# Two-layer diffusion trunk on one core: pairing a wide expert and a small expert in one slot-by-slot visit

## The chip, the cores and the metric

One program runs on one core of a Trainium2 chip. The metric is device time in microseconds (us) from the start to the end of an execution. Where the profile speaks of a span, it means the time from the first to the last recorded instruction of one profiled execution.

## The reference, cut to what matters

Two layers of a backbone over 128 context and 256 latent tokens (384 rows of 1024 values, float32). Each layer has a mixing part and a channel part. The channel part of layer 0 is a dense SwiGLU; that of layer 1 sends every row to 2 of 8 experts. Only the experts are touched here:

```python
def moe_swiglu(h, router, w_gate, w_up, w_down):
    probs = jax.nn.softmax((h @ router).astype(jnp.float32), axis=-1)
    top_p, top_i = lax.top_k(probs, TOP_K)          # TOP_K = 2 of 8
    top_p = top_p / jnp.sum(top_p, axis=-1, keepdims=True)
    combine = ...                                    # weight of each expert for each row
    a = jnp.einsum('bsd,edf->bsef', h, w_gate)       # 1024 x 1408 for each expert
    u = jnp.einsum('bsd,edf->bsef', h, w_up)
    hid = jax.nn.silu(a) * u * combine[..., None]
    return jnp.einsum('bsef,efd->bsd', hid, w_down)  # 1408 x 1024
```

An expert has 3 x 1024 x 1408 float32 weights, 17.30 MB. Eight of them are 138.4 MB, and each is read once in this run.

## The kernel before, in words

**The stages.** The kernel runs the mixing part and the dense channel part of layer 0, the mixing part of layer 1, then routes the rows and runs the experts, and at the end gathers each row's two results, sums, scales and stores them. The experts take the last quarter of the span. TensorE (PE) does the products into eight PSUM banks; ScalarE (ACT) and VectorE (DVE) prepare operands and empty banks; SyncE's queue (SP) issues the loads of weights; GpSimd (POOL) scatters the rows to `xslots` in DRAM and gathers them from `yslots`.

**Wide and small visits.** A wide visit takes up to 128 rows of one expert, a small one ("side" in the code) up to 64. `VISITS` (L50) lists the first visits as pairs (wide item, small item):

```python
VISITS = ((0, None), (None, 0), (1, 1), (None, 2), (2, 3))
```

So the order is: wide 0 alone; small 0 alone, with an expert of its own; wide 1 together with small 1, which are two batches of rows of the same expert; small 2 alone; wide 2 together with small 3. After these come wide 3, 4 and 5 in a loop on every engine. `BY_RANK` (L59) gives each expert a place by the number of its rows: the two least used experts go to the visits that are only small, and two busy ones get a wide and a small place. In this run there are six wide and four small batches of rows.

**Slots.** The weights of a visit come in ten slots (j = 0 to 9), each a load of at most 2 MB (2048 KB). Slots 0 to 5 hold gate and up (`M_GU` = 6): two slots for each of three blocks of columns, 512, 512 and 384 wide. Slots 6 to 9 hold down (`M_DN` = 4): 6 or 5 tiles of 128 rows by one half (512) of the 1024 output columns. The weights live in five places (`M_SLOT` = 5), four in `ring` and one in `oT`; slot j sits in place j mod 5, and SP waits until the use of slot j - 5 is over before it issues the load of slot j (L855 to L875, through `used_in`, L831, and `m_used`, L702). SP works in order: what it waits for holds up all later loads.

**A wide slot.** Products of a wide visit take three passes of reduced float32: `m_upper` (L712, ACT) writes the upper part of the weights to one of two tiles, `w_upper_a` and `w_upper_b`; `m_lower` (L718, DVE) writes the rest over the raw weights in their place; `product` (L1634) has PE multiply upper by upper, upper by lower and lower by upper. A slot's work on ACT and DVE goes in parts (`M_PART`); `ahead` (L2140) makes the upper part of slot j + 2 once slot j has been multiplied. `gate_silu` (L2135, ACT) and `hidden_gate` (L2811, DVE) form the hidden values of a block, `turn_hidden` (L1708, PE) turns them, `hidden_upper` (L2130) and `hidden_lower` (L2804) split them. `gathered` (L2124 and L2781) splits the rows of the next visit, which `next_rows` (L1683, PE) has turned.

**A small slot.** `side_slot` (L1646) multiplies by the raw float32 weights, without a split, two groups of 64 PE columns side by side. `side_silu`, `side_gate`, `side_turn` and `side_copy` (L2156, L2786, L1674, L2163) form and turn its hidden values. In a shared visit the small batch uses a slot's raw weights two slots ahead of the wide batch, since DVE overwrites them afterwards (`half_lower`, L2816, waits for the small batch's use).

**Order on the engines.** There is no scheduler: each engine's order is written by hand, in `side_visit` and `main_visit` (L1695 and L1717) for PE, `side_visit` and `item_upper` (L2179 and L2197) for ACT, `side_visit` and `item_lower` (L2794 and L2821) for DVE. Each engine executes in its order and waits at semaphores. A visit's result goes from PSUM to `ytok` by `out_half` (L2147, ACT) in two halves, and SP stores it when it comes to `store_out` (L820), at slot 5 of the next visit. Right before the first small load, SP waits for the scatter of the rows (`moved`, L849).

Of the kernel before, what the change touches and what calls it, by code (L numbers as in the profile page):

```python
# [28 lines left out]
P = 128  # L29
# [20 lines left out]
VISITS = ((0, None), (None, 0), (1, 1), (None, 2), (2, 3))  # L50
# [8 lines left out]
BY_RANK = ((0, None), (1, 1), (2, 3), (3, None), (4, None), (5, None), (None, 2), (None, 0))  # L59
# [122 lines left out]
def build(nc, cst_d, x_prompt, x_sample, cache_k, cache_v, state_in, c, c_ctx, ada_w, ada_b, norms, w_in, qk_norm,  # L182
# [3 lines left out]
    with ctx:  # L186
# [199 lines left out]
        side_x, side_ht = v3(H[:, 0:SIDE * KT], KT), v3(H[:, 512:512 + SIDE * FE], FE)  # L386
        side_h, side_sg, side_xs = H[:, 1216:1472], H[:, 1472:1728], H[0:SIDE, 1728:1728 + D]
# [62 lines left out]
        GU_BANK, TURN_BANK, OUT_BANK = ((0, 1), (6, 7), (0, 1)), (2, 3, 2), (3, 2)  # L450
        SIDE_ROWS, SIDE_DOWN = 6, (7, 6)
# [3 lines left out]
        turns = []  # L455
        for v, (item_v, side_v) in enumerate(VISITS):
            n_item, n_side = VISITS[v + 1] if v + 1 < len(VISITS) else (FIRST, None)
            rows_v = ["rows"] if n_side is not None else []
            hidden_v = [(side_v, b) for b in range(3)] if side_v is not None else []
            turns += hidden_v[0:2] + [("rows", n_side)] * len(rows_v) + hidden_v[2:] if item_v is None else hidden_v + [("rows", n_side)] * len(rows_v)  # L460

        def side_bank(s, b):

            alone = [item for item, x in VISITS if x == s][0] is None
            return B[((0, 1, 0) if alone else (4, 5, 4))[b]]
# [9 lines left out]

        def turned(*key):

            return FG + turns.index(key) + 1
# [4 lines left out]

        def following(v):

            return VISITS[v + 1] if v + 1 < len(VISITS) else (FIRST, None)

        def rows_in_by(v):

            n_item, n_side = following(v)  # L490
            items = [x for x, _ in VISITS[1:v + 1] + ((n_item, n_side),) if x is not None]
            sides = [x for _, x in VISITS[1:v + 1] + ((n_item, n_side),) if x is not None]
            return 16 * len(items) + 16 * len(sides)

        def visit_of(i):

            return VISITS.index([x for x in VISITS if x[0] == i][0]) if isinstance(i, int) and i < FIRST else i + NE - N_FIX
# [149 lines left out]
        slots = []  # L647
        for item_v, s in VISITS:
            if item_v is None:
                slots += [(s, j) for j in range(M_GU + M_DN - 1)] + [(s + 1, 0), (s, M_GU + M_DN - 1), (s + 1, 1)]  # L650
            elif s is not None:
                slots += [(s, j) for j in range(2, M_GU + M_DN)]

        def m_place(j, split=False):

            if j % M_SLOT == M_SLOT - 1:
                return (otS if split else OT)[:, 0:SLOT]
            k = slot(U_MOE + j % M_SLOT)
# [3 lines left out]
        M_PART = ((1, 1, 2), (2, 2), (2, 2), (2, 2), (2, 2), (2, 2), (3, 3), (3, 2), (3, 3), (3, 2))  # L662
# [9 lines left out]
        def m_shape(j):  # L672

            return (2, 4, 512 if j < M_GU - 2 else 384) if j < M_GU else (1, 6 - j % 2, 512)

        def m_first(j):

            return 4 * (j % 2) if j < M_GU else 6 * (j % 2)
# [33 lines left out]
        def m_upper(act, j, h, i):  # L712

            if h == 0:
                act.wait_ge(m_sem(j), m_full(j, visit_of(i)))
            nc.scalar.activation(m_half(w_upper[j % 2], j, h), m_half(m_place(j), j, h), ACT.Copy).then_inc(mw_hi, 1)  # L716

        def m_lower(eng, op, j, h, i, done):  # L718

            eng.wait_ge(mw_hi, M_IT * i + parts_to(j) + h + 1)  # L720
            op.tensor_tensor(m_half(m_place(j, True), j, h), m_half(m_place(j), j, h), m_half(w_upper[j % 2], j, h).bitcast(F32),  # L721
# [9 lines left out]
        def m_sem(j):  # L731
# [2179 lines left out]
```

## Time and profile before

| what | value |
|---|---|
| median of 3 runs | 1925.7 us (1922.33 to 1929.22) |
| profiled execution, its own time | 1921.34 us |
| its span | 1919.5 us |
| mean granted TensorE clock | 0.971 |
| PE busy | 1785.3 us (93%) |
| DVE busy | 1002.3 us (52%) |
| ACT busy | 787.2 us (41%) |
| POOL busy | 257.6 us (13%) |
| chain that ended last | PE 81%, ACT 5%, DVE 5%, DMA 5% |

The profiled execution lies 4.4 us under the median of the runs. Outside the span lie 1.8 us. Busy time of an engine is an average over stages; the trace can be asked for single stretches, given in us from the start of the span.

### The profile page before, as it was taken

The page shows a single profiled execution, that of the slowest core. Times are in us where ns is not written, and L with a number is a line of the kernel's source. Part 1 is how long each engine was busy: PE and PEld are TensorE (multiplying, and loading weights), DVE is VectorE, ACT ScalarE, POOL GpSimd, SP SyncE. Part 2 cuts the span into 40 slices and gives each one's busy share as a digit, 9 for nine tenths or more (in the row PEclk, how much of TensorE's full clock was granted, in tenths as well). Part 3 has the DMA queues.
Part 4 walks back from the last instruction along what each step waited for, and adds up shares of the span by engine and source line. Part 5 has one row for each costly group of instructions (what it writes and reads, how often), then busy time and mean ns, then how long its engine had stood idle before and what let it go on. Part 6 is the DMA issues. An engine that isn't in the chain of part 4 may idle for free.

```text
span 1919.5 us, 32369 instructions
## 1 busy us (share of the span) xinstructions
PE 1785.3 (93%) x14036; PEld 1503.8 (78%) x14036; DVE 1002.3 (52%) x1290; ACT 787.2 (41%) x1094; POOL 257.6 (13%) x221
## 2 busy tenths in 40 slices
PE   5999899999989999998998999999988799899994
PEld 3888688887869999877997788888867356468884
DVE  2866345444745443337963445546448044257885
ACT  3345622234344222224365422325345143347774
POOL 2610033231000000005300223320002000000001
PEclk9999899999999999998999999999999999899997
DMA  9652052216552344337521412226458978959994
GB/s 350 221 196 94 1 210 67 89 46 209 176 197 71 126 131 131 132 135 259 209 88 50 165 64 93 89 89 219 172 212 297 376 253 287 373 191 335 374 381 146
DMA packets 186387, 350.74 MB, mean 183 GB/s; under 512 B 5097, under 2 KB 60417, under 8 KB 185744
## 3 DMA queue, kind: packets, MB, share of 16 engines
q1 hardware_dynamic: 182464, 335.01, 49.5%
q0 software_dynamic: 3792, 13.80, 2.0%
q8 instruction: 104, 1.70, 0.4%
q14 instruction: 27, 0.22, 0.0%
HBM read 319.43 MB, written 29.36 MB: 182 GB/s over the span
## 4 chain that ended last, share of the span: by engine, by line
PE 81%; ACT 5%; DVE 5%; DMA 5%; SPq 2%; issue 2%; POOL 0%; POOLq 0%; DVEq 0%; ACTq 0%
PE bank L1100 6%; PE bank L1671 5%; PE bank L1102 5%; PE bank L1101 5%; PE bank L1640 5%; PE bank L1641 5%; PE bank L1643 5%; PE bank L1528 3%; PE bank L1526 3%; PE bank L1527 3%; PE bank L1136 3%; PE bank L1138 3%; PE bank L1137 3%; PE bank L1341 2%; PE bank L1478 2%
## 5 line engine op out<-in xcount | busy, mean ns | idle before, releaser
L1102 PE MATMUL bank<-hT_hi,ring_split 128*128 128x384 f32 x576 | 196.1, 340 | 0.0
L1777 ACT ACTIVATE ring_split<-ring 128x1024 fp32r<-128x1024 f32 (+2 forms) x84 | 119.5, 1440 | 180.1 <-DMA ring<-in_ffn_w_up 102.5
L2635 DVE TENSOR_TENSOR ring_split<-ring,ring_split 128x2048 fp32r<-128x2048 f32 (+1 forms) x28 | 73.9, 2670 | 142.7 <-ACT ring_split L1777 142.7
L1100 PE MATMUL bank<-hT_hi,ring_split 128*128 128x384 f32 x384 | 142.4, 371 | 4.3 <-DVE modv L2306 2.9
L721 DVE TENSOR_TENSOR ring_split<-ring,w_upper_a 128x1536 fp32r<-128x1536 f32 (+2 forms) x54 | 96.5, 1814 | 76.9 <-PE bank L1671 68.7
L1138 PE MATMUL bank<-ring_split,hT_hi 128*128 128x256 f32 x480 | 135.6, 283 | 0.0
L1101 PE MATMUL bank<-hT_lo,ring_split 128*128 128x384 f32 x384 | 130.9, 341 | 0.0
L1671 PE MATMUL bank<-ring,hT 128*64 128x256 f32 (+1 forms) x592 | 110.4, 513 | 17.6 <-DMA ring<-in_moe_w_up 14.0
L1528 PE MATMUL bank<-hT_hi,ring_split 128*128 128x384 f32 x352 | 118.8, 337 | 0.0
L1526 PE MATMUL bank<-hT_hi,ring_split 128*128 128x384 f32 x352 | 117.6, 334 | 0.0
L1527 PE MATMUL bank<-hT_lo,ring_split 128*128 128x384 f32 x352 | 117.2, 333 | 0.0
L721 DVE TENSOR_TENSOR ring_split<-ring,w_upper_b 128x2048 fp32r<-128x2048 f32 (+2 forms) x48 | 93.3, 1955 | 37.0 <-PE bank L1671 24.6
L1850 ACT ACTIVATE gates<-bank 128x384 f32<-128x384 f32 (+1 forms) x60 | 30.7, 512 | 197.6 <-PE bank L1102 163.2
L1102 PEld LDWEIGHTS bank<-hT_hi,ring_split 128*128 128x128 f32 x576 | 110.5, 192 | 0.0
L1136 PE MATMUL bank<-w_gran,hT_hi 128*128 128x256 f32 x384 | 107.0, 279 | 1.3 <-ACT ktok L1777 1.3
L1137 PE MATMUL bank<-w_gran,hT_lo 128*128 128x256 f32 x384 | 107.9, 281 | 0.0
L2380 DVE SCALAR_TENSOR_TENSOR conv<-gates,rowsT,conv 128x388 f32<-128x388 f32 x96 | 102.8, 1071 | 3.4
L1671 PEld LDWEIGHTS bank<-ring,hT 128*64 128x64 f32 x592 | 43.2, 143 | 73.3 <-issue 43.7
L716 ACT ACTIVATE w_upper_a<-ring 128x1536 fp32r<-128x1536 f32 (+2 forms) x54 | 81.6, 1533 | 45.5 <-PE bank L1643 26.1
L1641 PE MATMUL bank<-ring_split,xg_hi 128*128 128x512 f32 (+1 forms) x240 | 91.7, 382 | 0.0
L1777 ACT ACTIVATE work<-bank 128x256 f32<-128x256 f32 (+1 forms) x101 | 39.9, 445 | 126.0 <-PE bank L1341 71.1
L1138 PEld LDWEIGHTS bank<-ring_split,hT_hi 128*128 128x128 f32 x480 | 90.1, 188 | 0.0
(427 smaller groups left out, 4406.1 us busy)
## 6 DMA issues: line engine op xcount, KB each, us to landing
ring<-in_w_in SPq DMA_DIRECT2D x28, 2048.0 KB, 9.0
ring<-in_ada_w SPq DMA_DIRECT2D x24, 2048.0 KB, 13.0
ring<-in_moe_w_gate SPq DMA_DIRECT2D x32, 1024.0 KB, 8.1
ring<-in_moe_w_up SPq DMA_DIRECT2D x32, 1024.0 KB, 10.3
ring<-in_moe_w_down SPq DMA_DIRECT2D x16, 1536.0 KB, 9.1
ring<-in_w_branch SPq DMA_DIRECT2D x8, 1536.0 KB, 12.4
ring<-in_ffn_w_gate SPq DMA_DIRECT2D x11, 1024.0 KB, 5.4
ring<-in_ffn_w_up SPq DMA_DIRECT2D x11, 1024.0 KB, 7.9
```

The lines of the kernel that those rows point to most:

```text
L721: op.tensor_tensor(m_half(m_place(j, True), j, h), m_half(m_place(j), j, h), m_half(w_upper[j % 2], j, h).bitcast(F32), ALU.subtract).then ...
L1100: mm(out, hi, hT_hi[:, k], start=k == 0, stop=False)
L1101: mm(out, hi, hT_lo[:, k], start=False, stop=False)
L1102: last = mm(out, lo, hT_hi[:, k], start=False, stop=k == KT - 1)
L1136: mm(out, hT_hi[:, k, ts], hi[k], start=k == 0, stop=False)
L1137: mm(out, hT_lo[:, k, ts], hi[k], start=False, stop=False)
L1138: last = mm(out, hT_hi[:, k, ts], lo[:, k], start=False, stop=k == KT - 1)
L1526: mm(out, w_hi(k), x_hi[:, k], start=k == 0, stop=False)
L1527: mm(out, w_hi(k), x_lo[:, k], start=False, stop=False)
L1528: last = mm(out, w_lo(k), x_hi[:, k], start=False, stop=k == n - 1)
L1641: mm(out, x_hi[:, k], lo[:, q, g], start=False, stop=False)
L1671: last = mm(out[CH[y], :, 0:w], x[:, kt], raw[:, q, :, 256 * y:256 * y + w], start=kt == 0, stop=kt == n_k - 1)
```

## The change

The list of visits becomes the following. A wide item with a small one, followed by a small one alone, is executed as one: "pair".

```diff
-VISITS = ((0, None), (None, 0), (1, 1), (None, 2), (2, 3))
+VISITS = ((0, None), (1, 0), (None, 1), (2, 2), (None, 3), (3, None))
-BY_RANK = ((0, None), (1, 1), (2, 3), (3, None), (4, None), (5, None), (None, 2), (None, 0))
+BY_RANK = ((0, None), (1, 0), (2, 2), (3, None), (4, None), (5, None), (None, 3), (None, 1))
```

Places of the same rows count as before: six wide, four small. In a pair PE takes, for each j, the wide slot j of the first expert, then the first small batch's slot j + 2 of the same weights, then slot j of the second expert for the second small batch:

```diff
+                    def pair_visit(i, v):
+                        a, c = VISITS[v][1], VISITS[v + 1][1]
+                        for j in range(M_GU + M_DN):
...
+                            if j in (2, 4):
+                                side_turn(a, j // 2)
+                            if j == M_GU:
+                                turn_hidden(M_BLK - 1, i)
...
+                            if j == M_GU + 2 and pair_next(v):
+                                next_side_rows(v)
+                            main_slot(j, i)
+                            if j in (2, 4):
+                                turn_hidden(j // 2 - 1, i)
+                            if j in (2, 4, 6):
+                                side_turn(c, j // 2 - 1)
+                            if j == M_GU + 1:
+                                pe.wait_ge(side_u, turned(c, 2))
+                                next_rows(v)
+                            if j == 0:
+                                side_turn(a, 0)
+                                side_slot(v + 1, 0)
+                                side_slot(v, 2)
+                            elif j < 8:
+                                side_slot(v, j + 2)
+                                side_slot(v + 1, j)
+                            elif j == 8:
+                                if pair_next(v):
+                                    side_slot(after(v), 0)
+                                side_slot(v + 1, 8)
+                                side_slot(v + 1, 9)
+                            elif pair_next(v):
+                                side_slot(after(v), 1)
```

The first two small slots of a pair stand in the visit before it (behind its wide slots 8 and 9). Loads follow the order of use, and each takes the place that was used five uses earlier, whatever its j:

```diff
+                for j in range(1, 8):
+                    slots += [(s, j + 2), (s + 1, j)]
+                    loads += [steps_v[j + 2], small_v[j]]
+                    freed_by += [steps_v[j], small_v[j]]
...
+        for n, (v, j) in enumerate(loads):
+            if n < M_SLOT:
+                x = n
+            else:
+                held_by[v, j] = freed_by[n - M_SLOT]
+                x = place_of[held_by[v, j]]
```

The down slots change their shape in every visit: 3, 3, 3 and 2 tiles of rows by all 1024 columns, where there were 6 and 5 tiles by half the columns, twice. The small down product takes 512 columns in an instruction where it took 256:

```diff
-        M_PART = ((1, 1, 2), (2, 2), (2, 2), (2, 2), (2, 2), (2, 2), (3, 3), (3, 2), (3, 3), (3, 2))
+        M_PART = ((1, 1, 2), (2, 2), (2, 2), (2, 2), (2, 2), (2, 2), (2, 1), (2, 1), (2, 1), (1, 1))
...
-            return (2, 4, 512 if j < M_GU - 2 else 384) if j < M_GU else (1, 6 - j % 2, 512)
+            return (2, 4, 512 if j < M_GU - 2 else 384) if j < M_GU else (2, min(3, FE - 3 * (j - M_GU)), 512)
```

With it both halves of a visit's result end with slot 9, so `out_half` moves for both halves behind the upper parts of the next visit's slots 0 and 1 (before, the first half was emptied after slot 7), and PE waits for them (`yt_ok`) ahead of slot 2, whose bank 6 the second half now uses:

```diff
                         act.wait_ge(ys_out, 32 * i + 1)
-                        out_half(0, i)
-                        if not last:
-                            for h in parts_of(0):
-                                ahead(M_GU + 2, h, i)
-                        out_half(1, i)
-                        if not last:
-                            for h in parts_of(1):
-                                ahead(M_GU + 3, h, i)
+                        if not last:
+                            for j in (M_GU + 2, M_GU + 3):
+                                for h in parts_of(j + 2 - M_GU - M_DN):
+                                    ahead(j, h, i)
+                        for half in range(2):
+                            out_half(half, i)
```

ACT and DVE get orders of their own for a pair. ACT's (DVE's is alike, with `lower` for `ahead_of`, `side_gate` for `side_silu`):

```diff
+                        side_silu(a, 0)
+                        ahead(0, 0, i)
+                        side_copy(a, 0)
+                        ahead(0, 1, i)
+                        gate_silu(0, i)
+                        ahead_of(1)
+                        side_silu(a, 1)
+                        side_silu(c, 0)
+                        side_copy(a, 1)
+                        ahead_of(2)
+                        hidden_upper(0, i)
+                        side_copy(c, 0)
+                        gate_silu(1, i)
+                        ahead_of(3)
+                        side_silu(a, 2)
+                        side_silu(c, 1)
+                        side_copy(a, 2)
+                        ahead(4, 0, i)
+                        hidden_upper(1, i)
+                        side_copy(c, 1)
+                        ahead(4, 1, i)
...
```

The rows of a pair's two small batches are loaded at once (128 rows, 512 KB, where there were two loads of 256 KB), and turned by eight transposes of 128 x 128 into banks 0 and 2 (`next_side_rows`), where there were eight of 64 x 64 for each batch. In the first visit SP now issues two loads of rows at slot 6 (wide 1's, by `rows_load`, and the small batches'), where it issued one. Each small result has a buffer of its own in turn (`side_y[s % 2]`) and is emptied by one ACT copy of 512 columns (`side_outs`) where there were two of 256; POOL waits for the store before (`side_out`) and stores it. Wide 3 gets a visit written out, ahead of the loop.

## Rows read from the trace of the kernel before

**Rows 1.** The page: busy us of each engine and its share.

```profile
PE 1785.3 (93%) x14036; PEld 1503.8 (78%) x14036; DVE 1002.3 (52%) x1290; ACT 787.2 (41%) x1094; POOL 257.6 (13%) x221
```

**Rows 2.** Busy time by stretch; columns as in the first row.

```profile
core 0: us, PE busy (x) PEld busy (x) DVE busy (x) ACT busy (x) POOL busy (x), PEclk, DMA share, GB/s
1431.00:1489.20 58.20, 50.09 (x229) 41.63 (x230) 47.44 (x71) 29.41 (x25) 11.59 (x6) 0.94 0.72 262
1489.20:1534.49 45.29, 33.87 (x188) 14.56 (x187) 2.62 (x6) 5.04 (x16) 0.00 (x0) 0.94 1.05 376
1534.49:1620.43 85.94, 85.94 (x440) 55.51 (x440) 42.12 (x31) 38.59 (x42) 2.44 (x4) 0.97 0.74 257
1620.43:1659.91 39.48, 31.68 (x187) 13.88 (x187) 2.62 (x6) 5.05 (x16) 0.00 (x0) 0.94 1.05 373
1659.91:1746.42 86.51, 86.51 (x440) 56.12 (x440) 46.22 (x36) 42.96 (x46) 2.31 (x4) 0.97 0.73 258
...
1794.70:1842.97 48.27, 47.97 (x230) 40.77 (x229) 42.18 (x30) 36.40 (x31) 0.00 (x0) 1.00 1.05 382
```

**Rows 3.** PE's waits from 1489 to 1746: us in total, times, longest.

```profile
PE bank L1671 <- DMA ring<-in_moe_w_up: 14.0, 3, 6.8
PE bank L1671 <- DMA ring<-in_moe_w_down: 3.5, 3, 1.7
```

**Rows 4.** Two stretches of 4 us in the gaps; columns as in rows 2.

```profile
1532.00:1536.00 4.00, 1.51 (x4) 0.53 (x6) 0.00 (x0) 1.53 (x2) 0.00 (x0) 0.54 1.06 389
1656.00:1660.00 4.00, 0.09 (x2) 0.09 (x4) 0.00 (x0) 0.11 (x1) 0.00 (x0) 0.50 1.06 389
```

**Rows 5.** PE in order of time: start, us, line, tiles, [idle before].

```profile
1472.15 0.71 PE L1692 MATMUL bank<-cst,hT 64*128 64x64 f32 x8
...
1534.49 5.97 PE L1671 MATMUL bank<-ring,hT 128*64 128x512 f32 x16 [5.91 <-DMA ring<-in_moe_w_up]
1540.29 2.32 PE L1671 MATMUL bank<-oT,hT 128*64 128x256 f32 x20
1542.45 3.60 PE L1671 MATMUL bank<-ring,hT 128*64 128x512 f32 x16
1545.98 0.50 PE L1640 MATMUL bank<-w_upper_a,xg_hi 128*128 128x512 f32 x1
...
1551.59 0.38 PE L1680 MATMUL bank<-cst,hT 128*128 128x128 f32 x2
...
1589.16 2.81 PE L1671 MATMUL bank<-ring,hT 128*64 128x256 f32 x24
...
1642.20 1.09 PE L1035 MATMUL bank<-cst,gates 128*128 128x128 f32 x8
...
1659.91 6.40 PE L1671 MATMUL bank<-ring,hT 128*64 128x512 f32 x16 [6.77 <-DMA ring<-in_moe_w_up]
```

**Rows 6.** ACT's and DVE's groups by form, 1489 to 1892: busy, mean ns.

```profile
L716 ACT ACTIVATE w_upper_b<-ring 128x2048 fp32r<-128x2048 f32 x20 | 37.7, 1912 | 10.8 <-PE bank L1643 10.1 <-DMA ring<-in_moe_w_up 0.7
...
L1777 ACT ACTIVATE ehid_hi<-bank 128x512 fp32r<-128x512 f32 x10 | 5.8, 576 | 0.0
...
L721 DVE TENSOR_TENSOR ring_split<-ring,w_upper_b 128x2048 fp32r<-128x2048 f32 x20 | 45.3, 2287 | 13.7 <-PE bank L1671 11.6 <-ACT w_upper_b L716 2.1
```

**Rows 7.** The page's DMA issues: KB each, median us to landing.

```profile
ring<-in_moe_w_up SPq DMA_DIRECT2D x32, 1024.0 KB, 10.3
```

**Rows 8.** The chain that ended last, in order of time, three pieces.

```profile
1518.35 16.09 DMA ring<-in_moe_w_up
...
1891.45 0.60 ACT gates L1777
1892.21 2.04 DMA yslots<-gates
```

**Rows 9.** SP's queue in order of time: the small batch's rows.

```profile
1464.05 0.56 SPq L829 DMA_DIRECT2D hT<-xslots  x1
```

**Rows 10.** SP's own waits: us in total, times, longest us.

```profile
SPq L849 <- DMA xslots<-hT,ktok: 21.2, 1, 21.2
```

More of the change, by code:

```diff
@@ L449, in y_of, with side_bank @@
             return banks[:, 512 * Y_BANK[t]:512 * Y_BANK[t] + D]
-        GU_BANK, TURN_BANK, OUT_BANK = ((0, 1), (6, 7), (0, 1)), (2, 3, 2), (3, 2)
-        SIDE_ROWS, SIDE_DOWN = 6, (7, 6)
+        GU_BANK, TURN_BANK, OUT_BANK = ((0, 1), (6, 7), (0, 1)), (2, 3, 2), (3, 6)
+        SIDE_BANK, SIDE_DOWN, ROWS_AT = (4, 5), (7, 1), (0, 2)
         side_mm, side_s, side_g, side_t, side_u, side_yt = gu_g, gu_s, gu_f, gu_u, gu_h, gu_hi
-        turns = []
+        gate_order, turns = [], []
         for v, (item_v, side_v) in enumerate(VISITS):
[L457 to L465, printed above, removed]
+            if item_v is not None:
+                if side_v is not None:
+                    both = [(side_v + a, b) for a, b in ((0, 0), (0, 1), (1, 0), (0, 2), (1, 1), (1, 2))]
+                    gate_order += both
+                    turns += both
+                next_v = v + 1 if side_v is None else v + 2
+                if next_v < len(VISITS) and VISITS[next_v][1] is not None:
+                    turns += [("rows", VISITS[next_v][1])]
+        def side_bank(s):
+            return B[SIDE_BANK[s % 2]]
         def side_cols(b, y):
@@ L645, in ff_part @@
             return 2 * FF_LOOP * it + 2 * j + g + 1 if it is not None else 2 * min(j, FF_GU) + max(j - FF_GU, 0) + g + 1
-        slots = []
-        for item_v, s in VISITS:
+        slots, loads, freed_by, late = [], [], [], []
+        for v, (item_v, s) in enumerate(VISITS):
             if item_v is None:
-                slots += [(s, j) for j in range(M_GU + M_DN - 1)] + [(s + 1, 0), (s, M_GU + M_DN - 1), (s + 1, 1)]
-            elif s is not None:
-                slots += [(s, j) for j in range(2, M_GU + M_DN)]
@@ new lines, in build @@
+        for v in range(len(VISITS), len(VISITS) + 2):
+            loads += [(v, j) for j in range(M_GU + M_DN)]
+            freed_by += [(v, j) for j in range(M_GU + M_DN)]
+        place_of, full_of, held_by = {}, {}, {}
+        filled_to = [full(U_MOE + x - NSLOT) for x in range(NSLOT)] + [0]
+        for n, (v, j) in enumerate(loads):
+            if n < M_SLOT:
+                x = n
+            else:
+                held_by[v, j] = freed_by[n - M_SLOT]
+                x = place_of[held_by[v, j]]
+            place_of[v, j] = x
+            filled_to[x] += 16 * (2 if j < M_GU else 1)
+            full_of[v, j] = filled_to[x]
@@ L1745, in main_visit @@
                         for j in range(M_GU, M_GU + M_DN):
[L1746 to L1751 removed]
+                            pe.wait_ge(hl_ok, M_BLK * i + min(j - M_GU + 1 if j > M_GU else 2, M_BLK))
@@ L2159, in side_silu @@
                         for ps, cs in side_pieces(b):
[L2160 removed]
+                            last = go(side_sg[s % 2][ps, cs], side_bank(s)[ps, cs], ACT.Silu)
                         last.then_inc(side_s, 1)
@@ L2200, in item_upper @@
+                    def item_upper(i, last, v=None):
                         for b in range(M_BLK):
@@ L2204, in item_upper @@
                                 hidden_upper(b - 1, i)
-                            if s is not None:
-                                side_copy(s, b)
                             if b < M_BLK - 1:
```

432 lines of the change are left out of this document (232 added, 200 removed).

## The prediction

> **What bounds the kernel now.** I read the page first: PE is busy 93% of the span and no other engine comes near [rows 1]. That is a mean, so next I cut the expert part, the only part that the change touches, into stretches [rows 2]. Four things are to be seen there. A wide visit by itself takes 48.27 us with PE busy for 47.97 and at full clock: PE bounds it, although DMA runs at 382 GB/s. The two visits that are only small (1489 to 1534, 1620 to 1660) have PE idle for 45.29 - 33.87 = 11.42 us and 39.48 - 31.68 = 7.80 us, DVE busy under 3 us, and DMA at 376 and 373 GB/s: the loads bound them. The two shared visits have PE never idle and DMA at 257 GB/s only. So the loads are short of time in one visit and have time left in the next. PE's waits say the same: 14.0 and 3.5 us for gate, up and down weights, and the longest, 6.8 us, is one for up [rows 3]. Last, the clock: after each long gap TensorE is granted its lower level of 1.2 GHz (the means of two stretches are 0.54 and 0.50 of 2.4 GHz) [rows 4], and the small slot behind the gap takes 5.97 and 6.40 us where the same slot takes 3.60 [rows 5].
>
> **The change part by part.** All sums are made against the profiled execution, 1921.3 us; the median of the runs is 4.4 higher. From the first small slot to the start of wide 3, 1489.20 to 1746.42, the kernel spends 257.2 us.
>
> 1. *PE's waits go.* 19.2 us of idle PE (11.42 + 7.80) [rows 2]. Whether they go depends on the loads in a pair. A step of a pair at slots 0 to 3 is one wide slot, 5.6 us (1545.98 to 1551.59), and two small ones of 3.6 us [rows 5], 12.8 us together. It needs two slots of 2.1 MB, 10.8 us at the 389 GB/s of [rows 4]. A whole pair needs 34.6 MB, 89 us at that rate, and has PE busy for some 115 us. So PE bounds the pair. The lead of a load: the place of the first expert's slot j + 2 comes free with the second expert's slot j - 2, 19.4 us of PE's time before use (wide j - 1, two small slots, wide j and a turn); a slot of the second expert takes the place of a wide slot and has 17.7 us. The median load of up lands 10.3 us after issue [rows 7]. So 7 us are left, and I put no stall down.
>
> 2. *The slow clock goes.* Clock deficit times length over the four stretches: 0.06 x 45.29 + 0.03 x 85.94 + 0.06 x 39.48 + 0.03 x 86.51 = 10.3 us of full-speed time [rows 2]. Of these, 1.2 and 2.0 us fall into the idle at the end of the two gaps (1532.0 to 1534.49 and 1656.0 to 1659.91, at about half speed [rows 4]); with some more just ahead of them I put 4 us down to idle that part 1 has counted, so 6.3 us are PE's own. As a check, the two first slots behind the gaps alone lost 2.4 and 2.8 us [rows 5].
>
> 3. *Small down products twice as wide.* Six row tiles by 256 columns take 2.8 us and five 2.3 [rows 5], so 10.2 us for a small batch's eleven tiles; at the 3.60 us for four tiles by 512 columns they take 9.9. Four batches: -1.0 us. Nothing hides it, PE being the bound.
>
> 4. *Rows of the small batches.* Before, four times eight transposes of 64 x 64, 0.71 us each time; after, twice eight of 128 x 128, 1.09 us each time [rows 5]: -0.6 us.
>
> 5. *Wide down slots in their new shape.* 66 products of 512 columns before and after, ACT and DVE parts over the same 11 x 1024 elements: nothing on PE. Slot 7 now needs only two blocks of the hidden values, slot 8 three, which is looser. The last slot shrinks from 15 products to 12, so the upper and lower parts of the next slot 0 have 0.7 us less: a part of 2048 elements takes 1.91 + 2.29 us [rows 6], and its use comes 5.5 us after its release. Nothing.
>
> 6. *The outputs and the added wait.* `out_half` moves behind the next visit's first two slots. Within visits PE's new wait ahead of slot 2 comes 10.9 us after the end of a visit, while ACT is through in 2 x 1.91 + 2 x 0.60 = 5.0 us: hidden. Behind that wait stand PE's whole order and, through it, SP's loads; if the cover failed, each of five visits would cost what ACT is late. At the very end there is no next visit: both copies follow the last product, one 0.60 us copy more ahead of the store that the chain runs through [rows 8]: +0.7 us.
>
> 7. *SP's and POOL's queues.* Before the first pair SP issues 1 MB of rows instead of 0.25 MB, after a wait of 21.2 us [rows 10], at 1464.05 [rows 9]; PE turned the rows at 1472.15 without a wait [rows 5]. The further bytes take 2 us and delay slot 7's load by as much; by the orders and durations of [rows 5, 6] DVE is still done with that slot about 0.7 us before PE wants it. Ends: 0, or 4 us if these rows have to share with the three down loads behind them. I take 1. Later rows are asked for some 50 us ahead. POOL's added wait for the store before it holds up only its own next store, one visit later. Issues of down loads stay four to an expert, all hidden.
>
> 8. *New waits in a pair.* The trace of before has no pair, so I followed the three orders with the durations of [rows 5, 6]. The tightest place is step 4: behind wide slot 4 ACT makes an upper part (1.91), a hidden copy (0.58) and `side_copy` of the second batch (no more than another 0.58), 3.1 us, while PE does two turns and a small down slot, 3.6 us; then PE needs that copy. 0.5 us are left there, 2 us or more elsewhere. Ends: 0 (no such wait), or, if every one of a pair's six turns of small hidden values makes PE wait for a chain of copy, gate and semaphores of about 1 us, 12 us. I take 1, near the lower end, since the shared visits, with the same chain, show PE never idle [rows 2].
>
> Sum: -19.2 - 6.3 - 1.0 - 0.6 + 0.7 + 1 + 1 = -24.4 us, 1896.9 us for the profiled kind of execution, 1901.3 for the median. Built up instead: 2 wide visits of 48.3, four small batches of 6 x 3.6 + 9.9 + 1.1 for turns, and 2.2 of rows make 229 us instead of 257, less by 28 before the waits and the tail: the two agree within 2 us.
>
> **The rivals.**
> *A, short chains eat a part.* Part 8 at its upper end and part 7 at 4: -24.4 + 11 + 3 = -10.4, 1915. For it: ACT's order is rigid, and 0.5 us of slack is little. Against: rows 2, as said.
> *B, loads still bound the pair in part.* If the rate in a pair stayed at 257 GB/s [rows 2], two experts would take 34.6 / 0.257 = 135 us instead of 115. Twice, +40 us. But 257 is what PE asked for; 373 to 389 GB/s is what the loads reach when asked [rows 2, 4]. At 300 GB/s it would be 115 us and cost nothing. As B I take half of the idle left, 10 us: 1911.
> The Trainium skill, in DMA: Bandwidth & Descriptors, section Specifications, gives a core some 358 GB/s of HBM as its limit. By it a pair would need 97 us, still under PE's 115, and a wide visit with its rows and results 51 us; this trace does not agree: it shows 382 to 389 GB/s and a wide visit of 48.27 us. So B keeps a small chance.
> *C, slower.* One mechanism: the turnaround of a place. A pair's loads each wait for one use on PE, so a load that lands later than its lead of 17.7 us stretches every step, the lead being two steps: stretch = (turnaround - 17.7) / 2, in 20 steps. The gain is gone at 24.4 / 20 = 1.2 us a step, a turnaround of 20.1 us; at 22 us it is 20 x 2.15 - 24.4 = +18.6, 1944. For it: one load did take 16.1 us [rows 8], when three were queued ahead. Against: in a pair at most two are queued, and the median is 10.3 [rows 7].
> *D, no change.* The idle only moves: the first visit's end and the wide visits behind the pairs run with DMA at 1.05 of its share [rows 2] and could take the stalls over. The two pairs load 69 MB in 230 us, so DMA has 50 us over and enters wide 3 with its places full. To come out within 0.3% a stall of 20 us would have to appear there.
>
> **How the numbers follow.** The forecast, parts 1 to 8, has 0.72: 1901.3, by itself from 1895 (no new waits, and a median closer to the profiled execution) to 1908. A 0.10, B 0.08, D 0.05, C 0.05. The range goes from 1893 to 1913: it takes in B and part of A, and leaves out C, D and the rest of A, about 0.17. About 0.3%, 5.8 us, is what a measurement of this kernel can tell from no change; A and B are still beyond it. Faster: 0.72 + 0.10 + 0.08 = 0.90. Within 0.3%: 0.05. Slower: 0.05.
>
> **What would show it.** In the changed trace: PE's waits for DMA in the pairs near zero; clock 1.00 from the first pair to the end; a first pair of about 115 us and a second of about 107; DMA near 300 GB/s in both; wide visits still 48.3 us; the small down slots at 0.9 us a tile. Wrong would be: PE waiting on ACT or DVE for hidden values of small batches by over 1 us a time (A), for loads in the pairs (B, C), or in wide 3 (D); a wide visit over 48.6 us would say that part 5 or 6 is wrong.

## The result and the profile after

| what | before | after |
|---|---|---|
| median of the runs shown with the result | 1927.46 us, 4 runs (1922.33 to 1930.29) | 1901.8 us, 4 runs (1899.17 to 1905.67) |
| ratio after / before, 95% interval | | 0.9869 (0.9847 to 0.989) |
| profiled execution, its own time | 1921.34 us | 1899.17 us |
| its span | 1919.5 us | 1897.3 us |
| mean granted TensorE clock | 0.971 | 0.974 |

The kernel is faster by 25.7 us between the medians and by 22.2 us between the two profiled executions. The forecast was 24.4 us. The page of the kernel after, its engines and its loads of up, answers to [rows 1] and [rows 7]:

```profile
PE 1780.5 (94%) x13844; PEld 1493.2 (79%) x13844; DVE 1002.7 (53%) x1290; ACT 784.7 (41%) x1090; POOL 257.0 (14%) x221
ring<-in_moe_w_up SPq DMA_DIRECT2D x26, 1024.0 KB, 9.6
```

Busy time by stretch, with the columns of [rows 2]. The first row is the first visit up to the first small slot, the second and third are the first and the second pair, the fourth is all from the first small slot to wide 3, the fifth and sixth are wide 3 and wide 4, and the last is wide 3 to 5:

```profile
1431.99:1489.69 57.70, 50.65 (x225) 42.33 (x226) 48.25 (x72) 31.60 (x29) 10.79 (x6) 0.91 0.72 271
1499.82:1613.51 113.69, 113.69 (x532) 62.98 (x530) 44.92 (x37) 42.62 (x56) 2.22 (x4) 1.00 0.87 310
1613.51:1719.59 106.08, 105.94 (x492) 60.15 (x491) 45.01 (x37) 38.13 (x52) 2.10 (x4) 1.00 0.90 319
1489.69:1719.59 229.90, 229.76 (x1064) 127.43 (x1064) 94.49 (x77) 86.83 (x110) 4.32 (x8) 1.00 0.89 317
1719.59:1770.58 50.99, 48.33 (x231) 40.53 (x229) 39.55 (x29) 36.19 (x31) 0.00 (x0) 1.00 1.04 390
1770.58:1819.55 48.97, 47.86 (x230) 40.71 (x229) 41.94 (x29) 36.08 (x31) 0.00 (x0) 1.00 1.02 375
1719.59:1868.70 149.11, 144.19 (x690) 122.09 (x689) 121.17 (x84) 104.76 (x90) 0.00 (x0) 1.00 0.92 343
```

The same two long stretches of the kernel before:

```profile
1489.20:1746.42 257.22, 237.99 (x1252) 140.07 (x1251) 93.58 (x79) 91.65 (x118) 4.75 (x8) 0.96 0.84 296
1746.42:1891.42 145.00, 144.10 (x690) 122.49 (x689) 123.77 (x85) 105.30 (x90) 0.00 (x0) 1.00 0.92 335
```

Read the first two numbers of a row together. Before, PE was idle for 257.22 - 237.99 = 19.2 us between the first small slot and wide 3; after, it is idle for 0.14 us. The mean granted clock went from 0.96 to 1.00. DMA no longer swings between 257 and 376 GB/s [rows 2]; it runs at 310 and 319 in the two pairs. PE's waits from 1489 to 1870 answer to [rows 3], and no wait for a load is left among them:

```profile
PE bank L1101 <- DVE gates L2912: 3.5, 4, 1.1
PE bank L1706 <- DVE ring_split L781: 1.4, 1, 1.4
```

The stretches add up to the difference of the spans:

| stretch | before | after | difference | the steps of the prediction |
|---|---|---|---|---|
| up to the first visit | 1431.11 | 1431.99 | +0.9 | none (not touched) |
| the first visit | 58.1 | 57.7 | -0.4 | part 7: +1 |
| first small slot to wide 3 | 257.2 | 229.9 | -27.3 | parts 1 to 4 -27.1, part 8 +1 |
| wide 3 to 5 | 145.0 | 149.1 | +4.1 | part 5, D: 0 |
| last product to the end | 28.1 | 28.6 | +0.5 | part 6: +0.7 |
| span | 1919.5 | 1897.3 | -22.2 | -24.4 |

Two rows of this table need care, since they do not hold the same work on both sides. In the kernel after, the first small slot stands ahead of wide 0's last slot, so the third row holds that wide slot, 3.0 us of PE, which before is in the second row:

```profile
1493.27 0.50 PE L1706 MATMUL bank<-w_upper_b,ehid_hi 128*128 128x512 f32 x1
...
1496.23 3.65 PE L1730 MATMUL bank<-ring,hT 128*64 128x512 f32 x16
```

With the same work on both sides the first visit is 2.6 us longer, and the rest up to wide 3 is 30.3 us shorter. Together they give the same -27.7 us.

So two questions were left for experiments: whether the gain comes from what the prediction said (idle and clock, not the shorter small slots), and what took back 4.1 us in wide visits that the change was expected to leave alone. A third came from the prediction itself: how near the change is to rival C, the turnaround of a place.

Times of whole executions scatter by some us, and the start of the experts alone lies anywhere between 1431 and 1443 us in the profiled executions. So below, beside the ratios, stands the **stage**: from the first product of the first visit to the start of wide 3. It takes 315.3 us before and 287.6 us after.

### The profile page after: what moved, and what is told of

It is laid out like the page before. It is cut to its first block, busy times and chain, and to the rows that moved or that the text cites. A ratio compares the mean times of both kernels' runs of the same rounds, so it can differ in the third digit from the quotient of the medians.

```text
span 1897.3 us, 31887 instructions
## 1 busy us (share of the span) xinstructions
PE 1780.5 (94%) x13844; PEld 1493.2 (79%) x13844; DVE 1002.7 (53%) x1290; ACT 784.7 (41%) x1090; POOL 257.0 (14%) x221
## 4 chain that ended last, share of the span: by engine, by line
PE 81%; ACT 6%; DVE 6%; DMA 5%; issue 2%; POOL 0%; SPq 0%; POOLq 0%; DVEq 0%; ACTq 0%
PE bank L1730 6%; PE bank L1166 6%; PE bank L1168 5%; PE bank L1167 5%; PE bank L1706 4%; PE bank L1709 4%; PE bank L1707 4%; PE bank L1594 3%; PE bank L1592 3%; PE bank L1593 3%; PE bank L1202 3%; PE bank L1204 3%; PE bank L1203 3%; PE bank L1407 2%; DMA ring<-in_ada_w 2%
## 5 line engine op out<-in xcount | busy, mean ns | idle before, releaser
L781 DVE TENSOR_TENSOR ring_split<-ring,w_upper_a 128x2048 fp32r<-128x2048 f32 (+2 forms) x54 | 95.9, 1814 | 66.2 <-PE bank L1730 41.5
L1168 PEld LDWEIGHTS bank<-hT_hi,ring_split 128*128 128x128 f32 x576 | 109.9, 191 | 0.0
L776 ACT ACTIVATE w_upper_a<-ring 128x2048 fp32r<-128x2048 f32 (+2 forms) x54 | 80.4, 1529 | 54.8 <-PE bank L1709 41.1
L1730 PE MATMUL bank<-ring,hT 128*64 128x512 f32 (+1 forms) x452 | 101.4, 572 | 0.1
L781 DVE TENSOR_TENSOR ring_split<-ring,w_upper_b 128x2048 fp32r<-128x2048 f32 (+2 forms) x48 | 85.0, 1797 | 15.7 <-ACT w_upper_b L776 9.7
L1166 PEld LDWEIGHTS bank<-hT_hi,ring_split 128*128 128x128 f32 x384 | 73.9, 192 | 13.8 <-issue 3.8
## 6 DMA issues: line engine op xcount, KB each, us to landing
ring<-in_ada_w SPq DMA_DIRECT2D x24, 2048.0 KB, 12.9
```

Source lines behind the costliest of these rows:

```text
L781: op.tensor_tensor(m_half(m_place(j, visit_of(i), True), j, h), m_half(m_place(j, visit_of(i)), j, h), m_half(w_upper[j % 2], j, h).bitcas ...
L1166: mm(out, hi, hT_hi[:, k], start=k == 0, stop=False)
L1168: last = mm(out, lo, hT_hi[:, k], start=False, stop=k == KT - 1)
L1730: last = mm(out[CH[y], :, 0:w], x[:, kt], part, start=kt == 0, stop=kt == n_k - 1)
```

## The experiments

**Lighter loads before and after.** Both kernels load only two of the four row tiles of gate and up in the visits that are small alone, and multiply these two twice, so the number of products stays. The hidden values of these experts are not the reference's.

```diff
-                        sp.dma_start(d[:, :, g], src).then_inc(m_sem(j), 16)
+                        ks = slice(0, 2 if light else k)
+                        sp.dma_start(d[:, ks, g], src[:, ks]).then_inc(m_sem(j), 16)
...
-                    moe_load(e, j)
+                    moe_load(e, j, VISITS[v][0] is None)
...
```

The kernel before with this edit:

> The kernel before, but the two visits that are only small load just two of the four row tiles of each gate and up slot (5.8 MB less each) and multiply those twice; PE's, ACT's and DVE's instructions stay the same, and the values of these two experts are not the reference's. Theory (the change's gain is the wait for loads plus the slow clock behind it): PE's waits for DMA in 1489 to 1746 fall from 18 us to under 2, the clock stays full, and the time falls by 19.2 + 6.3 = 25 us, to 1902. Rival (the gain comes from the new order and shapes of instructions and loads, not from the bytes of these visits): within 5 us of the kernel before, 1927.

Measured: 1911.3 us, ratio to before 0.9919 (0.9891 to 0.9947); the stage takes 299.8 us, 15.5 less. The stretch from the first small slot to wide 3, PE's waits in it, and the two small slots behind the gaps that are left:

```profile
1495.39:1736.28 240.89, 234.54 (x1252) 139.31 (x1251) 93.58 (x79) 91.69 (x118) 4.77 (x8) 0.98 0.78 272
```

```profile
PE bank L1672 <- DMA ring<-in_moe_w_up: 6.3, 2, 3.3
```

```profile
1529.93 4.98 PE L1672 MATMUL bank<-ring,hT 128*64 128x512 f32 x16 [3.09 <-DMA ring<-in_moe_w_up]
...
1649.59 6.58 PE L1672 MATMUL bank<-ring,hT 128*64 128x512 f32 x16 [3.26 <-DMA ring<-in_moe_w_up]
```

In this stretch idle PE fell from 19.2 to 6.35 us, by 12.9, and the time by 16.3. So loads were the cause, and idle costs more than its own length, as said. But the run falls short of the full gain that was expected (1902 us). A third of the idle stayed, at the first slot of the next visit, whose own loads are of full size. And the clock did not come back in proportion. Behind a gap of half the length, the second slot takes 6.58 us, as long as the 6.40 behind 6.77 us of waiting [rows 5]; the first takes 4.98.

The kernel after with the same edit:

> The changed kernel with the same lighter loads for the second expert of each pair (values of these two experts are not the reference's). Theory (PE bounds the pairs): the pairs keep their length within 1 us; in all at most 2 us faster than the changed kernel's 1902, by the 1.4 us that PE waits in wide 3. Rival B (loads still hold the pairs up in part): 5 us or more faster, 1897 or less.

Measured: 1905.38 us, 0.9894 (0.986 to 0.9929); the stage takes 286.6 us against 287.6.

```profile
1491.31:1721.31 230.00, 229.67 (x1064) 127.31 (x1063) 94.49 (x77) 86.83 (x110) 4.32 (x8) 1.00 0.77 269
```

With 15% less to load (269 GB/s instead of 317) the stretch takes 230.00 us instead of 229.90. Bytes do not bound the pairs, PE does, and rival B falls.

**Products in the gaps.** The kernel before, with 16 products of the identity, whose result nobody reads, between small slot 8 and the next batch's slot 0 in a visit that is small alone. Loads and waits stay; PE has 3.84 us of work in the gap.

```diff
+                            if j == M_GU + 2:
+                                for _ in range(16):
+                                    mm(B[3][:, 0:P], ident, ident, start=True, stop=True)
```

> The kernel before, with 16 matmuls of 128x128 into a bank that is free (some 4 us) put into each of the two long gaps, ahead of the first slot of the next visit; nothing else. Theory (the clock behind the gap is a cost by itself): the small slot behind the gap takes 3.6 us instead of 5.97 and 6.40, the gaps still end with their load, and the time falls by up to 2.4 + 2.8 = 5.2 us, to 1922. Rival (the clock does not depend on these gaps, or the extra work is in the way): no change or up to 2 us slower.

Measured: 1925.95 us, 0.9981 (0.9959 to 1.0002), which says nothing by itself; the stage takes 311.5 us, 3.9 less (some 5 were expected). The two slots behind the gaps, and the clock in 4-us stretches at the first gap:

```profile
1546.81 5.35 PE L1671 MATMUL bank<-ring,hT 128*64 128x512 f32 x16 [2.18 <-DMA ring<-in_moe_w_up]
...
1671.08 3.65 PE L1671 MATMUL bank<-ring,hT 128*64 128x512 f32 x16 [2.21 <-DMA ring<-in_moe_w_up]
```

```profile
1544.00:1548.00 4.00, 1.82 (x12) 0.82 (x12) 0.00 (x0) 1.21 (x2) 0.00 (x0) 0.93 1.05 387
1548.00:1552.00 4.00, 4.00 (x16) 1.23 (x14) 0.00 (x0) 2.59 (x2) 0.00 (x0) 0.64 1.05 387
```

With the gap of 6.77 us cut to 2.21, the second slot runs at full speed: 3.65 us where it took 6.40. So this slow slot was the clock's doing and not the loads'. At the first gap, just as short, the clock still fell, and it fell after PE had gone back to work (0.93, then 0.64). The term is real and is tied to idle PE, but filling part of a gap does not hold the clock for certain.

**Parts of the wide down slots.** In the kernel after, slots 6 and 8 are prepared as one tile of rows and then two, instead of two and then one:

```diff
-        M_PART = ((1, 1, 2), (2, 2), (2, 2), (2, 2), (2, 2), (2, 2), (2, 1), (2, 1), (2, 1), (1, 1))
+        M_PART = ((1, 1, 2), (2, 2), (2, 2), (2, 2), (2, 2), (2, 2), (1, 2), (2, 1), (1, 2), (1, 1))
```

> The changed kernel with the parts of wide slots 6 and 8 as (1, 2) tiles instead of (2, 1). Theory (in a wide visit alone, the first part of slot 6 now has 2048 elements and must wait for all of slot 4, which makes DVE late for the last hidden gate, PE waits 1.1 us instead of 0.5): PE's wait for DVE's gates falls to about 0.5 us a visit, the period of a wide visit from 49.0 to 48.3 us, in all 2 to 3 us faster than the changed kernel, 1899. Rival (the 0.7 us come from the order of the outputs or from the loads): the period stays at 49.0.

This edit came from PE's waits above: in each wide visit of the kernel after, PE waits 1.1 us for `gates`, the last block of hidden values, where it waited 0.3 before. ACT and DVE of wide 4 in the kernel after show why:

```profile
1797.51 2.86 ACT L776 ACTIVATE w_upper_a<-ring 128x2048 fp32r<-128x2048 f32 x2 [2.30 <-PE bank L1709]
```

```profile
1799.46 3.43 DVE L781 TENSOR_TENSOR ring_split<-ring,w_upper_a 128x2048 fp32r<-128x2048 f32 x2 [2.46 <-ACT w_upper_a L776]
1802.80 0.68 DVE L2906 TENSOR_TENSOR ehid_lo<-bank,ehid_hi 128x512 fp32r<-128x512 f32 x1
1803.40 0.55 DVE L2912 TENSOR_TENSOR gates<-bank,gates 128x384 f32<-128x384 f32 x1
```

And ACT at the same place before:

```profile
1819.46 1.49 ACT L716 ACTIVATE w_upper_a<-ring 128x1536 fp32r<-128x1536 f32 x1 [0.23 <-PE bank L1643]
1821.50 1.49 ACT L716 ACTIVATE w_upper_a<-ring 128x1536 fp32r<-128x1536 f32 x1 [0.55 <-PE bank L1643]
```

Before, slot 6's first part was 1536 elements wide, no wider than half of slot 4 of 3072 (384 columns), whose tile it overwrites: ACT wrote it as soon as PE was through the first half of slot 4. The new first part is 2048 wide and so needs PE to be through all of slot 4. ACT waits 2.30 us, both parts follow at once, DVE has 3.43 us of them in a row, and its gate of the last block ends late. Measured with one tile first (1024 elements): 1903.33 us, 0.9879 (0.9852 to 0.9907); wide 3 to 5 take 147.0 us instead of 149.1. Wide 4, and PE's waits in the three visits:

```profile
1771.49:1819.77 48.28, 47.98 (x230) 40.64 (x229) 41.99 (x29) 36.09 (x32) 0.00 (x0) 1.00 1.03 385
```

```profile
PE bank L1706 <- DVE ring_split L781: 1.5, 1, 1.5
PE bank L1101 <- DVE gates L2912: 1.1, 4, 0.3
```

A wide visit is back at 48.28 us from 48.97, and the longest wait for `gates` at 0.3 from 1.1. The cause is settled by these rows. The same wait costs 0.5 us in the first visit, where PE waits 1.0 us for `gates` after and 0.5 before. In whole executions the edit can't be told from the kernel after (their intervals overlap almost wholly).

**The turnaround of a place.** The kernel after, with the loads of the pairs waiting for a later use than the one that frees their place. All products and bytes stay.

```diff
+                waits_for[v, j] = freed_by[n - M_SLOT + (1 if v in (1, 2, 3, 4) and n > 2 * M_GU + M_DN else 0)]
...
-                v0, j0 = held_by[v, j]
+                v0, j0 = waits_for[v, j]
```

One use later, in all slots of the pairs but the first seven loads of the first:

> The changed kernel, but in the pairs SP issues each load one use later than it could (as if a place came free one use later); nothing else. The lead of a load falls from 17.7 to 19.4 us to 10.5 to 13.6 us. Theory (the loads have some 7 us to spare in a pair, landing about 10 us after issue): no more than 8 us slower than the changed kernel, since 10.5 us is just about a load's time. Rival C (a place's turnaround already is near the lead): each step stretches by 3 us or more, 60 us slower.

Measured: 1924.47 us, 0.9995 (0.9974 to 1.0017); the stage takes 308.0 us, 20.4 more. In whole executions nothing that can be told is left of the gain. At most 8 us had been expected: the expectation failed. PE's waits, in total, and the first two in order of time:

```profile
PE bank L1731 <- DMA ring<-in_moe_w_up: 6.5, 1, 6.5
PE bank L1731 <- DMA oT<-in_moe_w_up: 4.0, 1, 4.0
PE bank L1731 <- DMA oT<-in_moe_w_down: 3.8, 1, 3.8
PE bank L1731 <- DMA ring<-in_moe_w_down: 1.5, 1, 1.5
```

```profile
1606.88 9.50 PE L1731 MATMUL bank<-ring,hT 128*64 128x512 f32 x36 [6.50 <-DMA ring<-in_moe_w_up]
...
1623.36 5.35 PE L1731 MATMUL bank<-oT,hT 128*64 128x512 f32 x16 [4.04 <-DMA oT<-in_moe_w_up]
```

Three of the four waits stand where one visit meets the next: at slots 0 and 1 of the second pair (the two rows) and at the last small slot 9 (3.8 us). The shortest, 1.5 us, is for the second expert's slot 6 in the second pair. Two uses later:

> The same with two uses later: leads of 4.5 to 6.4 us in the pairs. Theory: under the 7 to 10 us that a slot takes from issue to landing, so PE waits at each slot 2 to 5 us, and the time rises by 60 to 120 us. If it rises by less than 30 us, loads land faster than I think and five places are more than the pair needs.

Measured: 2029.78 us, 1.0532 (1.0462 to 1.0602); the stage takes 414.0 us, 126.4 more, a little above the 60 to 120 expected. The stretch again:

```profile
1488.94:1846.17 357.23, 265.50 (x1064) 133.36 (x1063) 94.26 (x77) 87.06 (x110) 4.30 (x8) 0.88 0.59 208
```

PE is idle for 91.7 us at 208 GB/s, at a clock of 0.88: neither PE nor DMA bounds this kernel, but the round trip from release through load to use. Of PE's 29 waits in the stretch 28 are for loads. This is the slower side that rival C named.

To see where the short leads are, the same delay was put on the inner loads alone (slots 4 to 9 of the first expert, 2 to 7 of the second), and then on the ten others, the seams (slots 0 to 3 of a first expert, 0, 1, 8 and 9 of a second). The first seven loads stay as they were both times:

```diff
+                inner = 4 <= j <= 9 if v in (1, 3) else 2 <= j <= 7
```

Inner loads:

> The changed kernel; only the loads of the inner steps of each pair (slots 4 to 9 of the first expert, 2 to 7 of the second) are issued one use later. Theory (inside a pair a load has 7 us to spare, and what was lost with all loads late was lost at the seam to the next visit): PE waits for DMA under 2 us in all, and the stretch from the first wide slot of the expert part to wide 3 stays at 287 us, within 2. Rival (the loss was spread over the steps): 300 us or more.

Seams:

> The complement: only the loads around the seams (slots 0 to 3 of the first expert, 0, 1, 8 and 9 of the second) are issued one use later. Theory: all of the loss is here; PE's waits for DMA of some 15 us come back and the same stretch takes 307 us. Rival: under 295.

Measured: inner 1910.07 us, 0.9904 (0.9866 to 0.9941), the stage 294.9 us (+7.3), with 5.3 us of waits for loads. Seams 1920.49 us, 0.9956 (0.9933 to 0.9978), the stage 306.1 us (+18.5), with these waits:

```profile
PE bank L1732 <- DMA oT<-in_moe_w_down: 4.7, 1, 4.7
PE bank L1732 <- DMA oT<-in_moe_w_up: 4.3, 1, 4.3
PE bank L1732 <- DMA ring<-in_moe_w_up: 3.3, 1, 3.3
```

Seams were expected at 307 us and came close; inner loads were expected to cost under 2 us and cost 7.3, and the two losses don't add up to the 20.4 of both together. Where only inner loads are late, the longest wait and one of 1.2 us still stand at seams:

```profile
1601.10 7.95 PE L1732 MATMUL bank<-ring,hT 128*64 128x512 f32 x36 [1.23 <-DMA ring<-in_moe_w_up]
...
1721.55 3.30 PE L1732 MATMUL bank<-oT,hT 128*64 128x512 f32 x8 [2.45 <-DMA oT<-in_moe_w_down]
```

These two loads, slot 0 of the second pair and the last small slot 9, wait for no later use in this run. They queue behind inner loads that were issued later, and land 11.1 and 9.2 us after their issue where it is 8.6 and 6.6 in the kernel after. So 3.7 of the 5.3 us of waits are at seams, and 1.6 at inner slots. The kernel after shows why. SP issues one load at a seam, and one of an inner step:

```profile
1532.54 0.44 SPq L871 DMA_DIRECT2D ring<-in_moe_w_up  x1
...
1589.33 0.46 SPq L871 DMA_DIRECT2D ring<-in_moe_w_up  x1
```

Their landings, in us after the issue (last column), the inner one first:

```profile
ring<-in_moe_w_up SPq DMA_DIRECT2D x1, 1024.0 KB, 10.6
...
ring<-in_moe_w_up SPq DMA_DIRECT2D x1, 1024.0 KB, 8.6
```

And PE's use of them: the second half of the first row is the slot loaded at 1532.54, the head of the second row the one loaded at 1589.33.

```profile
1544.81 7.08 PE L1730 MATMUL bank<-ring,hT 128*64 128x512 f32 x32
...
1599.10 7.95 PE L1730 MATMUL bank<-ring,hT 128*64 128x512 f32 x36
```

The lead of a load is the time from its issue to its first use. The inner load has 1548.3 - 1532.5 = 15.8 us and lands after 10.6. The load at the seam has 1599.10 - 1589.33 = 9.8 us and lands after 8.6, with 1.2 us to spare. It is slot 0 of the second pair's wide expert, which takes the place of the first pair's wide slot 7 and is first wanted by the small batch only one wide slot and some small ones later. With one use of delay it is issued at 1595.87, lands 11.0 us later, and PE starts at 1606.88: this is the wait of 6.50 us.

The tightest load of the kernel after is another one at a seam, the last small batch's slot 9. It is issued when slot 7 has been used and is wanted one wide slot and one small one later:

```profile
1708.20 0.37 SPq L874 DMA_DIRECT2D oT<-in_moe_w_down  x1
...
1714.87 1.94 PE L1730 MATMUL bank<-oT,hT 128*64 128x512 f32 x8
```

It has a lead of 6.7 us and lands after 6.6. In the kernel after with lighter loads PE waits 0.3 us for this slot, and in the last run below 0.6 us.

**The last down loads.** The kernel after, with the down slots of the last small batch's expert cut to one tile of rows each, multiplied over and over; these down products are not the reference's.

```diff
-                moe_load(expert_of[v], j, v)
+                moe_load(expert_of[v], j, v, v == 4 and j >= M_GU)
```

> The changed kernel, with the four down loads of the last small batch cut to one row tile of 512 KB each (its values are not the reference's; the instructions of the engines stay). Theory (wide 3 takes 51.0 us instead of 49.0 because its slot 2 queues behind the last down loads, DMA being at full rate from 1708 on): wide 3 takes 49.0 to 49.6 us. Rival (slot 2 is late because its place comes free late, whatever is in the queue): 51 us still.

Measured: 1905.76 us, 0.9881 (0.985 to 0.9912). The question was why wide 3 takes 50.99 us, 2.0 more than wide 4 and 5. PE's waits in wide 3 to 5 are the same as in the kernel after:

```profile
PE bank L1102 <- DVE gates L2913: 3.5, 4, 1.1
PE bank L1707 <- DVE ring_split L781: 1.4, 1, 1.4
```

Wide 3 took 51.0 us here too, as the rival had it. So the time is not lost by queueing behind the last pair's down loads. In the kernel after, the load of its slot 2 is issued at 1715.70, lands 11.9 us later at 1727.6, and ACT, DVE and PE follow it:

```profile
1727.73 3.72 ACT L776 ACTIVATE w_upper_a<-ring 128x2048 fp32r<-128x2048 f32 x2 [2.47 <-DMA ring<-in_moe_w_up]
...
1732.12 0.47 PE L1706 MATMUL bank<-w_upper_a,xg_hi 128*128 128x512 f32 x1 [1.42 <-DVE ring_split L781]
```

Three slots of wide 3 are asked for within 4.5 us (1712.50 to 1717.04), because the pair's last uses follow each other closely; each then takes its turn at about 390 GB/s. That fits, and so does this: in the kernels whose pairs were stretched by one use of delay wide 3 takes 48.9 to 49.1 us. It was not tried by freeing a place earlier, and stays argued.

**Both remedies.** The kernel after with the parts of above, and with the last result's second half copied by DVE beside ACT's first:

```diff
+                    v.tensor_copy(ytok[:, 512:1024], B[OUT_BANK[1]][:, :]).then_inc(yt_ok, 1)
```

> The changed kernel with the parts (1, 2) of wide slots 6 and 8, and with the second half of the very last result copied by DVE beside ACT's first half. Theory: wide visits alone at 48.3 us and the end 0.5 us earlier, so 2.7 us in all from the first wide slot to the end of the span against the changed kernel, 1899. Rival: within 1 us of the changed kernel.

Measured: 1901.93 us, 0.9861 (0.984 to 0.9881). It is as fast as the kernel after, within what can be told, and not the 1899 expected. Wide 4 and 5 keep the gain of the parts (48.4 us each), but wide 3 took 51.5 us, with two waits for `ring_split` where there was one (2.5 us in all). From the last product to the end it is 29.0 us, not less than 28.6.

In the chain that ended last DVE's copy takes 0.70 us where ACT's first copy took 0.61. Behind the copy that chain runs in both kernels through SP's issue of the first half's store (0.37 us) to the second store. In the kernel after ACT's second copy ends at 1869.82 and SP's issue at 1869.88, so taking out the copy alone gives next to nothing, and the edit also has SP wait for both copies ahead of the first store. The second store starts 1.5 us after the last product, against 1.4 in the kernel after; the store that ended the kernel before started after 0.8. No version measured beats the kernel after by more than the measurement can tell; the one with the parts alone is 2.9 us shorter in its profiled execution from the start of the experts to the end (462.4 against 465.3 us), 1.3 of them in the first visit, where the clock was 0.94 against 0.91.

## Why the prediction was right, and where it was not

**Parts 1 to 4, right in mechanism, low in size.** Sum -27.1; the row of the table says -27.3, but with the same work on both sides it is -30.3. PE's idle went down by 19.1 of 19.2 us. Its busy time went down by 237.99 - 229.76 = 8.2 us, with wide 0's last slot left out by 11.2, against 6.3 + 1.0 + 0.6 = 7.9 for clock and shapes. How the 3.3 us more split between the two was not taken apart. The agreement to 0.2 us is luck. The two pairs take 113.7 and 106.1 us where 115 and 107 were expected. A small down tile takes 0.88 us:

```profile
1703.45 1.94 PE L1730 MATMUL bank<-ring,hT 128*64 128x512 f32 x8
1705.21 2.75 PE L1730 MATMUL bank<-oT,hT 128*64 128x512 f32 x12
```

Here two tiles start 1.76 us ahead of the next three. The light loads and the products in the gaps bear out the mechanism: the loads made PE idle, and idle PE made slots behind it slow.

**Part 5, "nothing", wrong.** It counted ACT's and DVE's elements, which stay, and looked at the release of slot 0's upper part. It did not ask on which of PE's products a part of 2048 elements has to wait when the slot it overwrites comes in halves of 1536. Measured: 0.7 us a wide visit, 2.1 in wide 3 to 5, given back by the edit of one line, and a wait 0.5 us longer in the first visit. The prediction's own sign for it, a wide visit over 48.6 us, showed it.

**Part 6, right in size.** +0.7 foreseen, +0.5 measured; there is no wait of PE for the outputs. At the end the second copy has company: SP's issue of the first store ends at the same time, as said above, and the part did not name it. **Part 7** put 1 us down. With the same work on both sides the first visit is 2.6 us longer, but PE waits for nothing new behind the loads of rows. 0.5 us is part 5's wait, and much of the rest goes with the clock of this execution: it was 0.91 against 0.94 before, and in the executions of the kernel after with lighter loads and with other parts, where it was 0.94 again, the same stretch takes 56.6 and 56.4 us instead of 57.7. **Part 8** put 1 us down for new waits. In the pairs there are no waits of PE for ACT or DVE at all; in the run with the other parts there is one of 0.5 us for a copy of ACT's. So the 0.5 us of slack at step 4 held, and rival A falls.

**Rival B** falls by the light loads. The rate of 358 GB/s of HBM for a core that the Trainium skill gives (DMA: Bandwidth & Descriptors, section Specifications) is passed again: wide 3 runs at 390 GB/s for 51 us.

**Rival C** did not happen, but its price was taken from the wrong place. Part 1 gave every load of a pair a lead of 17.7 or 19.4 us and left "7 us" to spare. Inside a pair the load looked at had 15.8 us and 5.2 of them to spare. At the seams the leads are 9.8 us for slot 0 of the second pair, with 1.2 us left, and 6.7 us for the last small slot 9, with 0.1 left. The point from which it decides was put at a turnaround of 20.1 us in 20 steps; in fact one use of delay at the seams alone, on ten loads (6.5 us for slot 0 of the second pair), costs 18.5 us.

**Rival D** came in small: wide 3 is 2.0 us longer than its neighbours, not 20. DMA does not enter wide 3 "with its places full", since the last places come free only with PE's last uses.

**The number.** 1901.3 us was forecast and 1901.8 measured. Between the profiled executions it is -24.4 against -22.2, and this nearness hides errors that cancel. From the first small slot to wide 3, with part 8's waits, the gain was 4.2 us larger than summed. The wide visits behind took 4.1 us that nobody counted, and the first visit 1.6 us more than part 7's. The medians are 25.7 us apart, which is the same within their scatter.

## What to carry to other kernels

Where one stage is short of bandwidth and its neighbour has some left, mixing their steps on one queue takes the idle away as long as each load's lead, from the release of its place to its first use, stays over its landing time. Work that lead out for every load, at the seams between groups first of all: a mean or a steady step hides the shortest, and a load can also be late because those queued ahead of it are. And when tiles change their shape, check each part against the boundaries of the part that it overwrites, not only the number of elements.

## What the runs showed of the hardware

- **Idle PE costs more than its length.** Per us of idle PE the stretch from the first small slot to wide 3 changed by 16.3 / 12.9 = 1.27 us with the light loads in the kernel before, and in the kernel after by 21.5 / 15.9 = 1.35 with loads one use later and by 127.3 / 91.6 = 1.39 two uses later. The rest goes with the granted clock: 1.00 over this stretch in the kernel after, 0.97 one use later and 0.88 two uses later.
- **The loss is not in proportion to the gap.** Slots of 3.60 us at full clock took 5.97 us after 5.91 of waiting and 6.40 after 6.77 [rows 5], but also 4.98 after 3.09, 6.58 after 3.26, 5.35 after 2.18, and 3.65 after 2.21. With loads two uses later one took 3.65 after 3.59. Why they differ was not tried.
- **The clock can fall when PE is busy again**: 0.93 in the 4 us in which the gap ended, 0.64 in the 4 us after it.
- **A landing takes what is queued ahead of it.** Loads of 1 MB of up landed 8.6, 10.6, 11.0 and 11.9 us after their issue in the rows above. The one of 8.6 took 11.1 in the run with late inner loads, where it was not held back itself but the loads ahead of it were issued later.
